# Two FFN input transposes moved from the output projection into the up projection of a decoder layer

## What is computed

```python
merged = jax.nn.sigmoid(parts['ga']) * (y_a @ w_proj_a) + jax.nn.sigmoid(parts['gb']) * (y_b @ w_proj_b)
x = x + ga1 * rms_norm(merged @ w_out, g_post_mix)
h = rms_norm(x, g_pre_ffn) * (1.0 + sc2) + sh2
gate, up = jnp.split(h @ w_up, 2, axis=-1)
x = x + ga2 * rms_norm((jax.nn.silu(gate) * up) @ w_down, g_post_ffn)
```

## Time and profile before

| | us |
|---|---|
| median of three runs (lowest, highest) | 1978.82 (1977.57, 1980.74) |
| the profiled execution's own time | 1981.02 |
| its span, first to last instruction | 1979.1 |
| PE busy | 1895.8 (96%) |
| DVE busy | 1119.8 (57%) |
| ACT busy | 720.0 (36%) |

### The profile page before, as it was taken

The page is one execution under the profiler, slowest core; times in us unless marked ns, Lnnn a source line. Parts: engine busy times, 40 slices in busy tenths (PEclk is TensorE's granted clock), DMA queues, the critical chain, the costliest instruction groups (busy, mean ns, idle before and its releaser), DMA issues.

```text
span 1979.1 us, 31109 instructions
## 1 busy us (share of the span) xinstructions
PE 1895.8 (96%) x11801; PEld 1485.0 (75%) x11801; DVE 1119.8 (57%) x2141; ACT 720.0 (36%) x1417; POOL 381.1 (19%) x482
## 2 busy tenths in 40 slices
PE   6999999998999999899999998899999999999998
PEld 3588878785666666566666776898999999888876
DVE  2444333475656565644312267888988888434354
ACT  2322210133434444412201047566565555323232
POOL 0000021132222222333000052000000000356653
PEclk8999999998999999999999999999999999999999
DMA  9344000013443000087534355333323333436453
GB/s 361 127 169 141 22 22 22 22 45 125 142 137 97 12 12 23 3 230 199 132 87 138 106 183 174 91 117 94 102 80 109 102 107 107 138 119 192 128 192 107
DMA packets 218528, 223.38 MB, mean 113 GB/s; under 512 B 11301, under 2 KB 186637, under 8 KB 215886
## 3 DMA queue, kind: packets, MB, share of 16 engines
q1 hardware_dynamic: 218382, 221.40, 36.4%
HBM read 209.02 MB, written 33.30 MB: 122 GB/s over the span
## 4 chain that ended last, share of the span: by engine, by line
PE 86%; DVE 5%; ACT 3%; issue 2%; DMA 2%; POOL 1%; SPq 0%; DVEq 0%; ACTq 0%; POOLq 0%
PE ps L2921 19%; PE ps L2822 12%; PE ps L2407 9%; PE ps L2675 5%; PE ps L2428 5%; PE ps L2863 5%; PE ps L2865 5%; PE ps L2864 5%; PE ps L2626 3%; PE ps L2665 3%; PE ps L2643 3%; DMA arena<-in_w_ada 1%; PE ps L2367 1%; DVE arena L2183 1%; ACT arena L1402 1%
## 5 line engine op out<-in xcount | busy, mean ns | idle before, releaser
L2921 PE MATMUL ps<-H_hi,W_hi 128*128 128x260 f32 (+1 forms) x1132 | 320.7, 283 | 9.4 <-DVE const L2252 9.4
L2921 PE MATMUL ps<-H_lo,W_hi 128*128 128x260 f32 (+1 forms) x1132 | 319.6, 282 | 0.0
L2921 PE MATMUL ps<-H_hi,W_lo 128*128 128x260 f32 (+1 forms) x1132 | 319.4, 282 | 0.0
L2921 PEld LDWEIGHTS ps<-H_hi,W_hi 128*128 128x128 f32 x1132 | 214.1, 189 | 11.1 <-issue 7.7
L1155 POOL CAST ra_hi<-arena 128x128 fp32r<-128x128 f32 (+2 forms) x112 | 58.9, 537 | 822.4 <-DVE W_lo L2191 470.0
L2191 DVE TENSOR_TENSOR W_lo<-arena,W_hi 128x512 fp32r<-128x512 f32 x276 | 190.1, 689 | 43.0 <-ACT W_hi L1425 40.6
L2921 PEld LDWEIGHTS ps<-H_lo,W_hi 128*128 128x128 f32 x1132 | 214.2, 189 | 0.0
L2921 PEld LDWEIGHTS ps<-H_hi,W_lo 128*128 128x128 f32 x1132 | 214.2, 189 | 0.0
L2407 PE MATMUL ps<-arena,hT 128*128 128x261 f32 (+2 forms) x768 | 194.5, 407 | 3.4 <-ACT hT L1203 2.5
L2863 PE MATMUL ps<-rw_hi,ra_hi 128*128 128x512 f32 x480 | 191.2, 398 | 6.8 <-DVE rw_lo L2039 6.7
L1425 ACT ACTIVATE W_hi<-arena 128x512 fp32r<-128x512 f32 x276 | 171.6, 627 | 67.6 <-PE ps L2921 60.5
(11 more groups left out here) (448 smaller groups left out, 3307.1 us busy)
## 6 DMA issues: line engine op xcount, KB each, us to landing
arena<-in_w_up SPq DMA_DIRECT2D x172, 256.0 KB, 3.1
hT<-in_w_down SPq DMA_DIRECT2D x65, 512.0 KB, 3.4
arena<-in_w_ada SPq DMA_DIRECT2D x12, 2048.0 KB, 8.1
arena<-in_w_out SPq DMA_DIRECT2D x24, 512.0 KB, 4.0
arena<-in_w_in SPq DMA_DIRECT2D x17, 512.0 KB, 4.2
past_cmp<-in_cache_cmp_kv SPq DMA_DIRECT2D x64, 128.0 KB
past_slc<-in_cache_slc_kv SPq DMA_DIRECT2D x64, 128.0 KB
arena<-past_cmp SPq DMA_DIRECT2D x8, 1024.0 KB, 6.3
```

The lines of the kernel that those rows point to most:

```text
L2921: ins = nc.tensor.matmul(out, a[:, k // 2, block], h[:, k, 0:w], start=(i in (0, 1, 3) and k == 0 and j == 0), stop=(k == 3 and j == 2), s ...
```

## The change

The transposes of tiles 4 and 5 and their scaling move from the last group of the output projection to places behind units 2 and 4 of the up projection (PE), and behind product 3 of units 3 and 5 (ACT). They use banks 4 and 5 there. Tile 3 stays where it was, and its scaling is now shared: four blocks by ACT, four by DVE. The up projection begins when tiles 0 to 3 are written, and no longer waits for tile 5. `H_sums` of the first call is cut in two: its first two sums stay behind the low part of step 17, the other two go behind the norms of tiles 3 and 4, ahead of the low part of step 20.

```diff
--- before.py
+++ after.py
@@ -1395,9 +1395,9 @@
                 nc.scalar.activation(junk[0:r, :], yt[0][n % 4][0:r, :], ACT.Square, accum_out=ss[0:r, n:n + 1]).then_inc(s_ss2, 1)
 
             def h2_act(n):
-                b = 4 if n >= 6 else 6
+                b = 4 if n >= 4 else 6
                 act.wait_ge(s_hT, n + 1)
-                for k in range(KD // 2 if n < 3 else KD):
+                for k in range(KD // 2 if n < 4 else KD):
                     for dst, a, z in h2_dest(n, k):
                         ins = nc.scalar.activation(dst, ps[:, b + k // 4, k % 4 * P + a:k % 4 * P + z], ACT.Identity,
                                                    scale=sc2[:, k, 0:1], bias=modT[:, 24 + k, 0:1])
@@ -1445,7 +1445,7 @@
                         x1_sq(mine[1])
                         x1_sq(mine[2])
                         rows_sqrt(3 + 2 * (g - 1), g - 1)
-                    if k >= 5:
+                    if k >= 5 and mine[k - 5] < 4:
                         h2_act(mine[k - 5])
 
             W_high(0, 0)
@@ -1487,8 +1487,8 @@
                     x1_sq({(3, 6): 6, (4, 3): 7, (4, 6): 8}[at])
                 if at == (5, 6):
                     rows_sqrt(7, 2)
-                if at in ((8, 3), (9, 3)):
-                    h2_act(at[0] - 2)
+                if at in ((3, 3), (5, 3), (8, 3), (9, 3)):
+                    h2_act({3: 4, 5: 5, 8: 6, 9: 7}[at[0]])
 
             for n in range(NU):
                 for i in range(7):
@@ -2133,15 +2133,17 @@
                                                       sc2[:, k, 0:1], modT[:, 24 + k, 0:1], ALU.mult, ALU.add)
                 ins.then_inc(s_hTd, 1)
 
-            def H_sums(half):
+            def H_sums(half, parts=(0, 1)):
 
                 dve.wait_ge(s_hTa, 3 + half)
-                dve.wait_ge(s_hTd, 3)
+                dve.wait_ge(s_hTd, 3 + half)
                 b11, t1, t2, b21, t3, b22, t4 = (x[:, :, half * P:(half + 1) * P] for x in H_src)
-                step(nc.vector.tensor_tensor(t1, t3, b11, ALU.subtract))
-                nc.vector.tensor_tensor(t2, b22, t1, ALU.subtract)
-                step(nc.vector.tensor_tensor(t3, b22, t3, ALU.subtract))
-                nc.vector.tensor_tensor(t4, b21, t2, ALU.subtract).then_inc(s_hsplit, 1)
+                if 0 in parts:
+                    step(nc.vector.tensor_tensor(t1, t3, b11, ALU.subtract))
+                    step(nc.vector.tensor_tensor(t2, b22, t1, ALU.subtract))
+                if 1 in parts:
+                    nc.vector.tensor_tensor(t3, b22, t3, ALU.subtract)
+                    nc.vector.tensor_tensor(t4, b21, t2, ALU.subtract).then_inc(s_hsplit, 1)
 
             def H_low(half, i):
                 dve.wait_ge(s_act, 7 * half + i + 1)
@@ -2219,13 +2221,12 @@
                         norm_x1(mine[0])
                         norm_x1(mine[1])
                     if k == 5:
-                        if g == 1:
-                            h2_dve(mine[0])
+                        h2_dve(mine[0])
                         norm_x1(mine[2])
                     if g == 1 and k > 5:
                         h2_dve(mine[k - 5])
-                    if g == 2 and k == 1:
-                        H_sums(0)
+                    if g == 2 and k in (1, 3):
+                        H_sums(0, (k // 2,))
                     if g == 2 and k >= 4:
                         for i in range(2 * k - 8, min(2 * k - 6, 7)):
                             H_low(0, i)
@@ -2887,8 +2888,8 @@
                 pe.wait_ge(s_xn2, n + 1)
                 if n:
                     pe.wait_ge(s_hTa, n)
-                    pe.wait_ge(s_hTd, min(n, 3))
-                b = 4 if n >= 6 else 6
+                    pe.wait_ge(s_hTd, min(n, 4))
+                b = 4 if n >= 4 else 6
                 for k in range(KD):
                     ins = nc.tensor.transpose(ps[:, b + k // 4, (k % 4) * P:(k % 4 + 1) * P], xn[:, n % 2, k * P:(k + 1) * P], ident)
                 ins.then_inc(s_hT, 1)
@@ -2899,7 +2900,7 @@
                     rows_step(0, g * KD + k)
                     if g == 1 and k == 0:
                         pe.wait_ge(s_mgdve, 24)
-                    if g and 3 <= k < 6:
+                    if g and 3 <= k < 6 and groups3[g - 1][k - 3] < 4:
                         h2_transpose(groups3[g - 1][k - 3])
 
                 for n in groups3[g]:
@@ -2922,7 +2923,8 @@
                                                stop=(k == 3 and j == 2), skip_group_check=True)
                 ins.then_inc(s_upps, 1)
 
-            pe.wait_ge(s_hTa, 6)
+            pe.wait_ge(s_hTa, 4)
+            pe.wait_ge(s_hTd, 4)
             for n in range(NU):
                 for i in range(7):
                     pe.wait_ge(s_wlo, MIX_W + 7 * up_of(n)[0] + i + 1)
@@ -2949,11 +2951,10 @@
                     if i == 6:
                         pe.wait_ge(s_updve, 5 * n + 2)
                     up_product(n, i)
-                if n == 7:
+                if n == 2:
                     pe.wait_ge(s_ytdve, 9)
-                    h2_transpose(6)
-                if n == 8:
-                    h2_transpose(7)
+                if n in (2, 4, 7, 8):
+                    h2_transpose({2: 4, 4: 5, 7: 6, 8: 7}[n])
                 if n == 9:
                     pe.wait_ge(s_xn2, 9)
                     pe.wait_ge(s_hTa, 8)
```

## The result

The changed kernel is slower: median 1987.48 us of seven executions (1981.41 to 1990.53) against 1980.74 for the kernel before, also of seven (1977.57 to 1981.81). The ratio is 1.0028, with a 95% interval of 1.0016 to 1.0040, so 3 to 8 us, or some 0.3%. A second session gave 1984.81 against 1980.58, ratio 1.0023 (1.0012 to 1.0035). The profiled execution took 1985.38 us, its span is 1983.6.

A forecast was written before the change was run, and what follows sets the result against it. ACT and DVE bound the stage change, DVE with PE just behind units 3 and 4, PE from unit 5. Terms -3.1 + 0.8 + 1.6 + 0.8 + 1.75 = +1.85 us on 1978.82 gave 1980.7, range 1976.0 to 1984.3.

The forecast's parts named there:

- the gain A: Output projection's end: step 23's low part, and so unit 0, starts 3.1 us earlier; bounds 2.1 to 3.8.
- B and D: Transposes of tiles 4 and 5 behind units 2 and 4 on PE: each adds 0.8 us.
- C, the block in unit 3: Tile 4's eight scaling instructions on ACT stall DVE 2.3 us, then PE: +1.6 us, bounds 0 and 2.75.
- E, the block in unit 5: Tile 5's scaling on ACT delays `up_copy` 0 and product 2 of unit 6: +1.75 us, bounds 0 and 2.75.
- The clock: Rival, chance 0.12: new PE waits in units 4 and 6 each bring half clock, 1.5 us twice; total +4.85, 1983.7 us.
- The absorbed rival: ACT stalls in units 3 and 5 cost nothing, unit 4's product 6 waits near 1.2: -1.5 us, 1977.3; chance 0.17.

The follow-up runs named there:

- the move alone: Changed kernel with tile 3 scaled on ACT alone and the four sums in one piece: 1987.38 us, ratio 1.0039 to before.
- late-loads experiment: "into the gaps" with unit 1's three w_up loads issued behind step 23's weights: 1977.78 us, ratio 0.9982 to before.
- the rearranged kernel: Changed kernel with transposes and scalings of tiles 4 and 5 kept in the output projection: 1978.42 us, ratio 0.9988 to before.
- the kernels with the blocks spread or cut: Changed kernel, tiles 4 and 5 scaled one instruction per product (1979.89 us, 0.9992), or cut to one of eight instructions each (1980.53 us, 1.0001).
- tile 4's block alone: Changed kernel with tile 5's scaling spread over products of units 5 and 6, unit 3's eight instructions kept: 1982.11 us, ratio 1.0017.
- filling the last of them: Changed kernel plus 16 transposes with unused results ahead of product 6 of unit 4: 1984.45 us, ratio 1.0015 to before.
- into the gaps: Changed kernel, tile 4 scaled behind step 23's high part, tile 5 transposed in unit 3's wait, scaled singly from unit 4: 0.9991, again 0.9990.

## Why the prediction was wrong

The forecast was +1.85 us and 1980.7; the measured median is 1987.48, above the range. The waits and stalls that it named came; the gain A was too large and the costs too small, one reading behind A was wrong, and a term that stood among the rivals belonged in the sum.

*A, the output projection: the landing was mis-sized.* Step 23's load was issued at 1217.37 (forecast 1217.4). It took 4.6 us to ACT's high part, not 3.9, so the lead was 2.3, not 3.1, inside the bounds given. The 3.9 was a misreading of rows 7, where falling traffic was taken for the load's landing. The DMA view of the kernel before, over 1218.1 to 1218.3, and of the changed kernel, over 1217.3 to 1217.5, has the time to landing:

```profile
arena<-in_w_out SPq DMA_DIRECT2D x1, 512.0 KB, 5.0
```

```profile
arena<-in_w_out SPq DMA_DIRECT2D x1, 512.0 KB, 4.6
```

So before, too, the load landed only about 1 us ahead of ACT's high part at 1224.24, and just that 1 us was ACT's to give; the move alone brought 0.9. The late-loads experiment shows what made the landing long: the three loads issued ahead of it.

*That the gain is the move's* was not said in the prediction, but A was summed as one. It is not: without the move 2.0 of it is there. ACT, busy 11.11 of 12 us, was late for step 23's weights by about 1 us only, and half a block (four instructions, some 1.4 us) less ahead of them was enough: in the rearranged kernel tile 4's scaling ends as they land. The other part of the gain is the earlier issue of the load (0.9 us), which the prediction put down to the cut of the sums. No run has the shared scaling without the cut sums, or the reverse, so this split is read from rows and not shown by a run.

*B and D, the transposes:* 0.87 each by the kernels with the blocks spread or cut, forecast 0.82. Right, and the place matters: ahead of product 6 of unit 3 one costs nothing.

*C, the block in unit 3:* 1.85, forecast 1.6. DVE's stall is 2.22 (forecast 2.3) and PE waits 0.17, 0.62 and 1.80 in unit 4. DVE did catch up 0.4, but not the 0.16 of the next unit. *E, the block in unit 5:* 2.0, forecast 1.75; product 2 of unit 6 waits for `up_copy` as said (1.08), product 1 for `up_add` (0.47).

Without the new stretches of half clock the sum is -2.3 + 0.87 + 1.85 + 0.87 + 2.0 = +3.3 us.

*The clock was the failing step.* The sum put the half clock behind the new waits at nothing. It stood as a rival with 0.12, with its price (1.5 for 3 us at half clock) and its place ("where the waits in unit 4 together come near 3 us"; they came to 2.6). It came in three of the four profiles that have these waits unfilled, for 1.6 us behind unit 4; that rival's second stretch, behind unit 6, came in none. Another 0.9 is in the slow stretch behind the old wait in unit 1 (13.2 for 12.3). That is not the change's: kernels with the same instructions up to there show 10.8, and the rearranged one, with the same wait of 3.4, shows 12.3. Sum: +3.3 + 1.6 + 0.9 = +5.8, which is what the profile shows at product 6 of unit 6. Rows 1 and 8 had shown one wait on this path that was paid twice, as idle time and in the clock behind it. New waits of 2.6 us should have carried a part of that in the forecast itself.

*The base.* The three executions shown had the median 1978.82; seven have 1980.74, and those of two further sessions 1981.12 (31) and 1980.58 (25). Of the 6.8 us between forecast and result 1.9 is this; 0.8 is A, 0.6 are the transposes and blocks, 1.6 is the new stretch and 0.9 the longer old one. About 1 us is left, and it stays open: the changed kernel's own two sessions differ by 2.7.

The absorbed rival fell: product 6 of unit 4 waited 1.80, not 1.2, and the blocks cost 1.85 and 2.0. On the rule that interleaving stages with different most-contended engines may help (the Trainium skill, Perfetto Trace Analysis, Optimization Strategy), the runs say: spread over the products, ACT's work does go into units 3 to 6 for 0.3 us or nothing, as the rule has it; in a block of eight, the same work on ACT, it doesn't.

Open: what decides whether the clock falls behind these waits. With tile 4's block alone they are the same and it did not fall in the one profile, so they don't bring the slow stretch every time. That filling the last of them took it away rests on one profile and on the ratio (1.0015 against 1.0028 and 1.0023, whose intervals overlap).

## What to carry to other kernels

Before moving work off a full engine, see whether that engine is on the path there or only busy ahead of someone else's wait: here ACT was late for a load by 1 us, and half a block less ahead of it was enough. Read a load's landing from the DMA view, not from where traffic thins. Where an engine hands on pieces with every product (1.4 us here), work put beside them goes in one instruction at a time, or into a wait that the profile shows; eight at once, 2.75 us, stalled the next engine for 2.2 and 2.8 us. A new wait of TensorE costs its idle time, and the half clock that may follow it (1.6 us in three profiles of four here) gets a term of its own in the sum.

## What the runs showed of the hardware

- One and the same program, the kernel before, takes 1976.7 to 1986.0 us; the mean granted clock of the executions goes with it (0.989 at 1976.95, 0.983 at 1984.58). Half a dozen slow stretches have fixed places (24, 36, 100, 448, 552, 1044 us); others, at 1228, 1244, 1260, 1300, 1340 and 1700, are there in some profiles and absent in others of a nearly equal program, at 1260 and 1300 even where the instructions up to there are the same. The two programs profiled twice (changed, into the gaps) show the same stretches both times.
- A wait of 3.2 to 3.4 us in unit 1 was followed by half clock in eight of thirteen profiles, and in five the clock stayed at 1.00 (for one, 1256 to 1264 in "into the gaps"). With transposes of unused results in that wait it stayed at 1.00 in the one profile there is.
- A load of 512 KB reached its consumer 3.5 us after its issue when issued ahead of three loads of 256 KB, and 4.9 behind them.
